# Attention scores in split float32r passes, the rope part as one stacked 128-row operand

## The reference

```python
def mla(h, cos, sin, w_down, q_norm, w_uq, kv_norm, w_ukv, w_o):
    down = h @ w_down
    c_q, c_kv, k_rope = jnp.split(down, [512, 512 + 256], axis=-1)
    q = (rms_norm(c_q, q_norm) @ w_uq).reshape(B, S, 8, 128 + 64)
    q_nope, q_rope = q[..., :128], apply_rope(q[..., 128:], cos, sin)
    k_rope = apply_rope(k_rope, cos, sin)
    kv = (rms_norm(c_kv, kv_norm) @ w_ukv).reshape(B, S, 8, 128 + 128)
    k_nope, v = kv[..., :128], kv[..., 128:]
    # for each block of 128 queries, keys up to the block's end, q scaled by 192 ** -0.5:
    s = einsum('bqhd,bkhd->bhqk', q_nope, k_nope) + einsum('bqhr,bkr->bhqk', q_rope, k_rope)
    p = softmax(where(mask, s, -inf))
    o = einsum('bhqk,bkhd->bqhd', p, v)
    return o @ w_o          # then h = h + mla(...)
```

## Time and profile before

| | |
|---|---|
| median of 3 runs | 1184.69 us (1183.39 to 1187.93) |
| span of the profiled execution | 1184.0 us, 19033 instructions |
| its mean granted TensorE clock | 0.983 |
| PE busy | 1116.5 us, 94% of the span, 7366 matmuls |
| DVE, ACT, POOL busy | 379.0, 272.9, 56.9 us |
| chain that ended last | PE 88%, DVE 5%, DMA 4% |

### The profile page before, as it was taken

How to read it: one execution, slowest core, us unless ns; L and a number is a source line. 1 busy time by engine, 2 the same in 40 slices (tenths; PEclk the granted TensorE clock), 3 DMA queues, 4 the chain that set the end, 5 groups by cost and what they waited for, 6 DMA issues and landing times.

```text
span 1184.0 us, 19033 instructions
## 1 busy us (share of the span) xinstructions
PE 1116.5 (94%) x7366; PEld 993.4 (84%) x7366; DVE 379.0 (32%) x691; ACT 272.9 (23%) x518; POOL 56.9 (5%) x99
## 2 busy tenths in 40 slices
PE   5989999999999999999997899999999999999980
PEld 4876666888888888888786899999999999999980
DVE  5555565354334443344474001010101010101015
ACT  5434443242224222242241001010101010101011
POOL 2201110000000000000002000000000000000002
PEclk9999999999999999999998999999999999999995
DMA  7016767425324154142203999999999999999996
GB/s 254 22 52 171 214 188 159 126 89 161 96 64 112 52 155 105 55 124 72 61 29 110 307 284 265 266 268 304 271 305 282 303 283 305 279 301 289 294 236 228
DMA packets 272652, 223.13 MB, mean 188 GB/s; under 512 B 29904, under 2 KB 245968, under 8 KB 272624
## 3 DMA queue, kind: packets, MB, share of 16 engines
q1 hardware_dynamic: 259616, 183.79, 55.8%
q0 software_dynamic: 11616, 36.32, 10.9%
q10 hardware_dynamic: 1392, 2.64, 0.6%
HBM read 196.33 MB, written 26.35 MB: 188 GB/s over the span
## 4 chain that ended last, share of the span: by engine, by line
PE 88%; DVE 5%; DMA 4%; issue 1%; ACT 1%; SPq 0%; POOL 0%; POOLq 0%; ACTq 0%; DVEq 0%
PE bank L1262 25%; PE bank L1276 13%; PE bank L869 13%; PE bank L871 13%; PE bank L870 13%; PE bank L1019 2%; PE bank L1018 2%; PE bank L1039 1%; PE bank L1323 1%; DMA stage_own<-in_moe_w_gate 1%; PE bank L881 1%; DMA stage_own<-in_moe_w_down 1%; PE bank L1166 1%; PE bank L1030 1%; PE bank L1251 1%
## 5 line engine op out<-in xcount | busy, mean ns | idle before, releaser
L1262 PE MATMUL bank<-scratch,stage_own 128*128 128x128 f32 (+1 forms) x2720 | 327.7, 278 | 4.6 <-DVE scratch L1742 1.6
L1262 PEld LDWEIGHTS bank<-scratch,stage_own 128*128 128x128 f32 x2720 | 318.3, 191 | 6.7 <-DVE scratch L1742 1.9
L1276 PE MATMUL bank<-qr_now,stage_own 128*128 128x128 f32 (+1 forms) x1152 | 143.6, 278 | 1.5 <-DMA stage_own<-in_moe_w_down 1.5
L1754 DVE TENSOR_TENSOR qr_now<-krT,bank 128x128 f32<-128x128 f32 (+1 forms) x80 | 23.3, 291 | 376.1 <-ACT krT L819 376.1
L1276 PEld LDWEIGHTS bank<-qr_now,stage_own 128*128 128x128 f32 x1152 | 137.3, 191 | 1.7 <-DMA stage_own<-in_moe_w_down 1.7
L869 PE MATMUL bank<-big_hi,w_lo 128*128 128x512 f32 (+2 forms) x352 | 134.4, 382 | 0.0
L871 PE MATMUL bank<-big_hi,w_hi 128*128 128x512 f32 (+2 forms) x352 | 134.3, 381 | 0.0
L870 PE MATMUL bank<-big_lo,w_hi 128*128 128x512 f32 (+2 forms) x352 | 134.2, 381 | 0.0
L1349 DVE TENSOR_TENSOR w_lo<-stage_own,w_hi 128x1024 fp32r<-128x1024 f32 (+1 forms) x91 | 105.4, 1202 | 12.0 <-ACT w_hi L587 11.9
L819 ACT ACTIVATE krT<-bank 128x128 f32<-128x128 f32 (+1 forms) x80 | 22.5, 281 | 374.6 <-PE bank L1262 374.6
L587 ACT CAST w_hi<-stage_own 128x1024 fp32r<-128x1024 f32 (+1 forms) x91 | 88.9, 1033 | 15.8 <-DMA stage_own<-in_mla_w_down 6.2
(11 more groups left out here) (234 smaller groups left out, 1103.8 us busy)
## 6 DMA issues: line engine op xcount, KB each, us to landing
stage_own<-in_moe_w_gate SPq DMA_DIRECT2D x82, 512.0 KB, 5.8
stage_own<-in_moe_w_up SPq DMA_DIRECT2D x82, 512.0 KB, 6.2
stage_own<-in_moe_w_down SPq DMA_DIRECT2D x72, 512.0 KB, 4.7
stage_own<-in_ffn_w_gate SPq DMA_DIRECT2D x21, 512.0 KB, 6.4
stage_own<-in_ffn_w_up SPq DMA_DIRECT2D x21, 512.0 KB, 7.0
stage_own<-in_ffn_w_down SPq DMA_DIRECT2D x21, 512.0 KB, 3.5
xbuf<-zeros POOLq DMA_DIRECT2D x2, 5184.0 KB, 40.7
scratch<-xbuf POOLq DMA_DIRECT2D x9, 576.0 KB, 6.9
```

The lines of the kernel that those rows point to most:

```text
L1262: last = t_.matmul(dst[:, 0:n], w[:, k * P:(k + 1) * P], xT[:, k, 0:n], start=k == 0, stop=k == KD - 1)
L1276: last = t_.matmul(bank[4 + k // 3][:, col:col + n], w[0:parts, k * P:(k + 1) * P], e_act[0:parts, par, 0:n], start=first and k % 3 == 0, ...
L1754: v.tensor_tensor(e_act[:, par, 0:n], e_silu[:, par, 0:n], bank[2 * par + 1][:, 0:n], ALU.mult).then_inc(prod_ready, 1)
```

## The change

The nope part of the scores becomes `mm3` on split operands: `qn_hi`, `qn_lo`, `kn_hi`, `kn_lo`. The rope part becomes two passes of 128 rows: `rotate_q` writes each head's rotated query twice side by side (`rotated[t]` is 1024 wide), a transpose of these 128 columns (`q2_T`, four transposes per head, in bank 4 behind `q_head`) gives the query doubled on 128 rows, of which `q2` keeps the rounded value on rows 0 to 63 and the remainder on rows 64 to 127. Multiplied with `kr_lo` and with `kr_hi`, both doubled, it gives all four partial products. `rope_T`, `qr_out` and the copies to `qr_now` go. `q_out` and `k_out` are now two steps each, hi on ScalarE and lo on VectorE, and so is the new `q2_out`; `q_head` waits for `q2_lo` of the head before, `q2_T` for `q_lo`, and the set-up ahead of attention does `k_head(0, 1)` before `q_head(0, 1)`.

The new operands lie over memory that exists: `qn_hi` to `kn_lo` over `h`, `q2` over the end of `big_hi`, `kr_hi` over `krT`, `kr_lo` over `qr_now`. So x no longer stays in `h`: GpSimd loads it again, four transfers of 512 KB (`x_again`), issued behind its stores of zeros once all scores are done, and `add_attention(t)` waits for its tile.

```diff
+        qn_hi, qn_lo, kn_hi, kn_lo = (over(name, [P, 2, S], "h", 2 * S * n)
+                                      for n, name in enumerate(("qn_hi", "qn_lo", "kn_hi", "kn_lo")))
+        q2 = over("q2", [P, 2, S], "big_hi", 6 * S)
+        kr_hi = over("kr_hi", [P, S], "krT")
+        kr_lo = over("kr_lo", [P, S], "qr_now")
...
@@ gpsimd, behind the three stores of zeros @@
+            pool.wait_ge(scores_done, H * T)
+            for t in range(T):
+                pool.dma_start(h[:, t, :], a["x"][0, t * P:(t + 1) * P, :]).then_inc(x_again[t], 16)
             pool.wait_ge(pv_done, H)
...
@@ scalar @@
             def q_out(pair, hd):
                 act.wait_ge(q_done, 2 * pair + (hd + 1))
-                s.mul(qn[:, hd, :], bank[4][:, :], SCALE).then_inc(q_ready, 1)
+                s.mul(qn_hi[:, hd, :], bank[4][:, :], SCALE).then_inc(q_hi, 1)
+
+            def k_out(pair, hd):
+                act.wait_ge(k_done, 2 * pair + (hd + 1))
+                s.copy(kn_hi[:, hd, :], bank[5][:, :]).then_inc(k_hi, 1)
+
+            def q2_out(pair, hd):
+
+                act.wait_ge(q2_done, 2 * pair + (hd + 1))
+                s.mul(q2[:, hd, :], bank[4][:, :], SCALE).then_inc(q2_hi, 1)
...
             c_hi(3)
-            qr_out(1)
-            qr_out(2)
+            act.wait_ge(xn_ready, T)
             q_out(0, 0)
-            qr_out(3)
-            act.wait_ge(qr_ready, T)
-            s.copy(qr_now[:, :], qrT[:, 0, :])
+            k_out(0, 0)
+            q2_out(0, 0)
             q_out(0, 1)
-            act.wait_ge(k_done, 2)
+            k_out(0, 1)
+            q2_out(0, 1)
             for j in range(2):
                 split("pair", j, 1)
...
@@ tensor @@
+            def q2_T(pair, hd):
+
+                pe.wait_ge(q_lo, 2 * pair + hd + 1)
+                for t in range(T):
+                    both = rotated[t][:, (pair * 2 + hd) * (2 * ROPE):(pair * 2 + hd + 1) * (2 * ROPE)]
+                    last = t_.transpose(bank[4][:, tok(t)], both, ident[:, :])
+                last.then_inc(q2_done, 1)
...
-            rope_T(0)
             latents_T(3)
-            rope_T(1)
             rope_q(3)
-            rope_T(2)
-            pe.wait_ge(qr_ready, 3)
+            pe.wait_ge(rope_ready, 3)
             q_head(0, 0, True)
             k_head(0, 0, True)
-            rope_T(3)
             values(0, True)
+            pe.wait_ge(rope_ready, T)
+            q2_T(0, 0)
+            k_head(0, 1)
             q_head(0, 1)
-            k_head(0, 1)
+            q2_T(0, 1)
...
-                        t_.matmul(dst[:, 0:n], qn[:, hd, tok(qb)], kn[:, hd, 0:n], start=True, stop=False)
-                        t_.matmul(dst[:, 0:n], qr_now[r, tok(qb)], krT[r, 0:n], start=False, stop=False)
+                        mm3(dst[:, 0:n], qn_hi[:, hd, tok(qb)], qn_lo[:, hd, tok(qb)], kn_hi[:, hd, 0:n], kn_lo[:, hd, 0:n],
+                            True, False)
+                        for kr in (kr_lo, kr_hi):
+                            t_.matmul(dst[:, 0:n], q2[:, hd, tok(qb)], kr[:, 0:n], start=False, stop=False)
...
@@ filler, place 1 and place 3 @@
                         k_head(pair + 1, 0)
+                        q2_T(pair + 1, 0)
...
                         k_head(pair + 1, 1)
+                        q2_T(pair + 1, 1)
...
@@ vector @@
+            def q_out(pair, hd):
+                dve.wait_ge(q_hi, 2 * pair + (hd + 1))
+                v.scalar_tensor_tensor(qn_lo[:, hd, :], bank[4][:, :], SCALE, qn_hi[:, hd, :], ALU.mult, ALU.subtract
+                                       ).then_inc(q_lo, 1)
...
             rotate_q(3)
+            q_out(0, 0)
             k_out(0, 0)
-            dve.wait_ge(ropeT_done, T)
             dve.wait_ge(v_done, 1)
             v_out(0)
             v_out(1)
+            q2_out(0, 0)
+            q_out(0, 1)
             k_out(0, 1)
+            q2_out(0, 1)
             for j in range(2):
                 split("pair", j, 1)
             dve.sem_inc(o_lo, 1)
...
             def add_attention(t):
+                dve.wait_ge(x_again[t], 16)
```

More of the change, by code:

```diff
@@ L246, in trunk @@
         x_landed = [sem(f"x_landed{t}") for t in range(T)]
+        x_again = [sem(f"x_again{t}") for t in range(T)]
         attn_gain_landed = sem("attn_gain_landed")
@@ L288, in trunk @@
         rope_ready = sem("rope_ready")
-        ropeT_done = sem("ropeT_done")
-        qr_ready = sem("qr_ready")
+        q2_done = sem("q2_done")
+        q2_hi = sem("q2_hi")
+        q2_lo = sem("q2_lo")
         q_done = sem("q_done")
@@ L628, in c_hi @@
                 s.copy(cqT_hi[:, :, tok], bank[2][:, :].rearrange("p (k n) -> p k n", k=4))
+                s.copy(kr_hi[:, tok], bank[3][:, 2 * P:3 * P])
                 s.copy(ckvT_hi[:, :, tok], bank[3][:, 0:2 * P].rearrange("p (k n) -> p k n", k=2)).then_inc(cT_hi, 1)
@@ L712, in attention @@
                 turned(0)
+                if more:
+                    k_out(pair + 1, 0)
+                    q2_out(pair + 1, 0)
                 head_out(0)
                 exps(1)
-                if more:
-                    s.copy(qr_now[:, :].unsqueeze(1), qrT[:, bass.ds(pair + 1, 1), :])
                 between(1)
@@ L720, in attention @@
                 turned(1)
+                if more:
+                    k_out(pair + 1, 1)
+                    q2_out(pair + 1, 1)
                 between(2)
@@ L963, in q_head @@
                 if not first:
-                    pe.wait_ge(q_ready, 2 * pair + hd)
+                    pe.wait_ge(q2_lo, 2 * pair + hd)
                 weights("pair", 0, pair)
@@ L971, in k_head @@
                 if not first:
-                    pe.wait_ge(k_ready, 2 * pair + hd)
+                    pe.wait_ge(k_lo, 2 * pair + hd)
                 weights("pair", 1, pair)
@@ L1060, in filler @@
                         k_head(pair + 1, 1)
+                        q2_T(pair + 1, 1)
                 return filler
-            with pe.Fori(0, H // 2 - 1) as pair:
+            for pair in range(H // 2 - 1):
                 attention(pair, next_pair(pair))
@@ L1451, in rotate_q, with q2_out @@
                 dve.wait_ge(rope_done, t + 1)
[L1452 to L1453 removed]
                 shape = "p (t h n) -> p t h n"
[L1455 to L1460 removed]
+                q, turned, tmp = (m.rearrange(shape, t=1, h=H) for m in (bank[rope_bank[t]][:, :], *rope_tmp))
+                product(turned, tmp, q, H, slice(t, t + 1))
+                both = rotated[t].rearrange("p (h two n) -> p h two n", h=H, two=2)
+                turned, tmp = (m[:, 0].unsqueeze(2).broadcast_to([P, H, 2, ROPE]) for m in (turned, tmp))
+                link(v.tensor_tensor(both, turned, tmp, ALU.add))
+                dve.sem_inc(rope_ready, 1)
+            def q_out(pair, hd):
+                dve.wait_ge(q_hi, 2 * pair + (hd + 1))
+                v.scalar_tensor_tensor(qn_lo[:, hd, :], bank[4][:, :], SCALE, qn_hi[:, hd, :], ALU.mult, ALU.subtract
+                                       ).then_inc(q_lo, 1)
+            def k_out(pair, hd):
+                dve.wait_ge(k_hi, 2 * pair + (hd + 1))
+                v.tensor_tensor(kn_lo[:, hd, :], bank[5][:, :], kn_hi[:, hd, :], ALU.subtract).then_inc(k_lo, 1)
+            def q2_out(pair, hd):
+                dve.wait_ge(q2_hi, 2 * pair + (hd + 1))
+                low = slice(ROPE, 2 * ROPE)
+                v.scalar_tensor_tensor(q2[low, hd, :], bank[4][low, :], SCALE, q2[low, hd, :], ALU.mult, ALU.subtract
+                                       ).then_inc(q2_lo, 1)
             def v_out(hd):
@@ L1524, in attention @@
                 between(0)
+                if more:
+                    q_out(pair + 1, 0)
                 turned(0)
@@ L1533, in attention @@
                 between(1)
+                if more:
+                    q_out(pair + 1, 1)
                 turned(1)
```

44 lines of the change are left out of this document (19 added, 25 removed).

## The result

The kernel after takes 1198.1 us in the median of 4 runs (1196.35 to 1199.78), the kernel before beside it 1186.03 us (1183.39 to 1187.93). The ratio is 1.0098, 95% interval 1.0081 to 1.0115: slower by 1%, 12 us. The forecast was 1194.5 us, range 1185 to 1202. The profiled execution has a span of 1198.2 us, 14.2 over the one before; it was the slowest of its four runs, and by the medians the loss is 12 us.

A forecast was written before the change was run, and what follows sets the result against it. TensorE was taken as the bound, busy 128.3 of 129.0 us between 88 and 217. Span 1184.0 + 8.2 (x reloaded behind the zeros) + 1.6 (slow clock) = 1193.8; median 0.7 over it, 1194.5 us, range 1185 to 1202.

The forecast's parts named there:

- two readings: GpSimd's DMA queue: works in order, so x cannot pass the zeros (chosen), or shares freely, x landing by 202 to 203.
- The scores: Attention, one head's scores: 3.6 us for 5.88, a gain of 2.25 a head, 18 for eight.
- Attention starts: TensorE's path after the changed set-up: attention starts 1.6 us later.
- The zeros start: GpSimd's first store of zeros goes out at 94.7 for 91.39, 3.3 us later, bounds 2.4 to 4.
- First pair: First two heads of attention: +0.4 us, the o_lo wait and the held division against the gain.
- Second and third pair: Middle four heads of attention on TensorE's path: -2.8 us for the second pair, -2.0 for the third.
- Fourth pair: Last two heads of attention: -3.7 us, so TensorE would end wo_part(1, 7) at 211.6.
- The three stores take as long as now: GpSimd's zeros keep their durations, plus or minus 2 us; their end moves from 220.2 to 223.5.
- x 1.5 behind the zeros, 1.4 to the restart: Behind attention: first x load lands at 225.1, additions take 1.29, TensorE starts at 226.5 for 218.31, +8.2 us.
- The clock: TensorE's restart after idling from 211.6 to 226.5: 3.1 us at half clock, half of it lost, +1.6 (0 to 3.4).
- The rival in which GpSimd can't issue x: Small loads on GpSimd are held too, x lands 3 to 4 us later: 1198 to 1200 us; chance 0.08.
- The one in which x is there in time: Queue shared, not in order: x there by 203, faster scores count, -6.5, 1178.2 us; chance 0.10.

The follow-up runs named there:

- the run without zeros: Kernel after with all three stores of zeros issued behind the loads of x and the gain: 1190.0 us, ratio 1.0029 to the kernel before.
- the run with the third store last: Kernel after with the third store of zeros (ybuf) issued behind the loads of x and the gain: 1183.7 us, ratio 0.9968.
- the zeros from 40: Kernel after without GpSimd's wait ahead of the zeros, the first store going out at about 40 in place of 95.3: 1202.3 us, ratio 1.0149.
- all zeros from the second head: Kernel after with GpSimd waiting for the second head's first score block before all three stores, still ahead of x: 1210.0 us, ratio 1.0197.

## Why the prediction was right, and where its sizes were off

The mechanism was the forecast one, and it set the time: x behind the zeros in GpSimd's queue, TensorE idle, the slow clock behind that. The order within the queue, on which I had to choose between two readings, is shown by two runs that take it away (x in 5.2 us with no store ahead; x ahead of the zeros from another queue) and by one that shifts it (the zeros end at 236.7, 9.2 us later, and the restart comes 9.2 us later). The 12 us of loss are the reload's: with the same scores and the third store out of the way the kernel is 0.3% faster than the kernel before, and with all stores well placed 0.9%. Step by step:

- *The scores*, 3.6 us a head: 3.64. *Second heads* of a pair: 1.8 forecast, 16.22 to 14.33, 1.9 gained. *First heads*: 0.3 to 1.0 forecast, 1.06 and 0.73 gained where nothing was held.
- *Attention starts* 1.6 later: 2.3. *The zeros start* 3.3 later: 3.9.
- *First pair* +0.4: +1.7. The division held by GpSimd's issue costs the first head 4.4 us, as the run without zeros shows, while the kernel before paid about 0.5 for its own (13.86 against 13.38 in the next first head). I had named the hold and priced it at too little; the slow clock behind it, 1.5 of the 4.4, stands nowhere in the prediction.
- *Second and third pair* -2.8 and -2.0: -3.0 and -2.6.
- *Fourth pair*: its 3.7 of gain missed the hold of the third issue, 2.1 us in the seventh head, which I had not counted. With the first pair this is why TensorE was through at 214.8, not at 211.6. It cost nothing here, since x came at 228.9 anyway.
- *The three stores take as long as now*: this term was off most. They kept the queue 132.2 us in place of 128.8, 3.4 us more where I had allowed 2. What made the second one 2.6 longer is open: from 136.6 to 180.8 SP's queue moved 3.33 MB, 3.01 before in the stretch that answers to it, which at the 200 GB/s of both explains 1.6 us of it; that was argued, not tried.
- *x 1.5 behind the zeros, 1.4 to the restart*: 1.4 and 1.4.
- *The clock* +1.6: 12 passes at 0.20 more, 2.4.
- *The median 0.7 over the span*: it is 0.1 under it, since the profiled execution was the slowest of its four. So the forecast of the median, 1194.5, is 3.6 short, that of the span 4.4.

Together: 0.6 + 3.4 - 0.2 for the restart (230.3 for 226.5) and 0.8 for the clock are 4.6, the distance from the forecast 1193.8 of span to 1198.2 within 0.2. The rival in which GpSimd can't issue x has its time (1198 to 1200) but not its cause: the four issues took 2.19 us. The one in which x is there in time (1178.2, a gain of 6.5) has its place in the run with the third store last: 1183.7 in the median, a gain of 4 us on the kernel before beside it.

What I had not seen is that the zeros can cost a reordered kernel in three ways: order in their own queue, VectorE's hold with the slow clock behind it, and weight loads beside them. The order alone turned the gain into a loss. With it gone 0.3% of gain are left, and the rest up to 0.9% came only when the first store neither held a softmax nor kept TensorE waiting for a load of w_uq. The kernel before gained nothing from the one other place that was tried for its zeros (0.9998).

## What to carry to other kernels

Before a load is added to a queue, write down what is in that queue at that moment and when its last byte lands; a store of 4.6 MB, itself issued late behind 10 MB of the same kind, turned a load of 5 us into one of 33. When a change gives up memory that was in place, price the reload with the stage that waits for it, and ask which operand needs that memory and for how long: here `rotated`, kept for all tiles through attention, pushed the queries and keys over `h`. And ask what each part brings: the stacked rope 2.06 of 2.24 us a head, the nope split 0.18. And place large background transfers by what they hold up (a softmax, small-packet loads with a deadline), not by when the issuing engine is free.

## What the runs showed of the hardware

- An issue on a hardware queue can hold the engine that makes it: ScalarE 13.4 us for three loads of 512 KB beside a store of zeros. TensorE waited 9.4 us for the work queued behind. SP is held as well, up to 19.9 us by one issue in the kernel after; what that costs, no run here separates.
- Loads in small packets can last until a large store beside them ends. Of the two w_uq loads of 256 KB that SP issues one behind the other, the first took 12.4 to 15.4 us and the second 22.0 to 27.2, in five cases from four runs (24.8 and 27.2 with the zeros from 40, 24.7, 25.9, 22.0), and each second one landed within 0.5 us of the store's end. The w_up load of 512 KB took 28.8 us and landed 1.3 after it. In the two kernels themselves, where the first store ended some 12 us after the issue, the second load took 12.6. With no store beside them the w_uq loads take 3.1 us (all zeros behind the gain). Beside the load of 28.8 us the queues moved, from 262 to 282:

```profile
q0 software_dynamic: 823, 3.21, 56.9%
q1 hardware_dynamic: 2548, 1.28, 21.6%
```

0.5 KB a packet against 3.9 KB. Why they last until the very end of the store, these runs leave open.
- The granted clock was 0.50 for 12 passes behind 15.5 us of idle time, for 12 again behind 4.5, for 14 behind 9.5 (all zeros behind the gain) and for 10 behind 28.7 (all zeros from the second head). So the price behind the idle time was 2.0 to 2.8 us and did not grow with its length. Short waits in a row can bring it too: in the first head of the kernel after the clock fell to 0.50 behind waits of 1.7, 0.7 and 0.5 us.
